# Weighting the one-hot rows of an expert router on ScalarE instead of VectorE, one block of eight tokens ahead

## The reference, cut to what matters

```python
q = (xt @ w_pq).reshape(T, PK_HEADS, 2, PK_DHALF)
s1, s2 = einsum('thd,hnd->thn', q[:, :, 0], k1), einsum('thd,hnd->thn', q[:, :, 1], k2)
t1, i1 = lax.top_k(s1, 16); t2, i2 = lax.top_k(s2, 16)
ts, ci = lax.top_k((t1[..., :, None] + t2[..., None, :]).reshape(T, 8, 256), 16)
e = take(i1, ci // 16) * 128 + take(i2, ci % 16)      # expert = (first key, second key)
g = softmax(ts)                                        # gate of each of the 128 choices
act = gelu(einsum('td,thkd->thk', xt, u_tab[e]))
out = einsum('thk,thkd->td', g * act, v_tab[e])
```

## Time and profile before

| what | us |
|---|---|
| runs of the kernel | 2574.62, 2577.2, 2577.13; median 2577.13 |
| the profiled execution: its own time | 2580.62 |
| the profiled execution: its span | 2578.8 |
| gate stage, from the first one-hot instruction of DVE to the last product of PE: from 1482 to 1864 | 382 |
| in it: busy time of DVE, PE, POOL, ACT | 377.6, 330.7, 215.5, 157.0 |
| down stage and end: from 1878 to 2579 | 701 |

### The profile page before, as it was taken

The page is one execution under the profiler, slowest core; times in us unless marked ns, Lnnn a source line. Parts: engine busy times, 40 slices in busy tenths (PEclk is TensorE's granted clock), DMA queues, the critical chain, the costliest instruction groups (busy, mean ns, idle before and its releaser), DMA issues.

```text
span 2578.8 us, 29605 instructions
## 1 busy us (share of the span) xinstructions
PE 2331.2 (90%) x11005; PEld 1786.0 (69%) x11005; DVE 1622.4 (63%) x2696; ACT 666.8 (26%) x1419; POOL 964.2 (37%) x552
## 2 busy tenths in 40 slices
PE   6699999899879999997897988888879999999996
PEld 6699977665457978997897888888834444444442
DVE  2376654444543222999889799999835555555555
ACT  2143520133322212242333344434300110001011
POOL 8455455400004424264656665555411111111110
PEclk9899999955689999998998999999989999999998
DMA  6323233300133213164666777777799999999994
GB/s 237 105 99 109 98 107 124 104 20 17 33 94 139 66 33 128 42 233 139 226 229 203 235 252 282 281 271 280 268 361 371 374 381 378 386 377 383 383 376 180
DMA packets 192546, 541.94 MB, mean 210 GB/s; under 512 B 17057, under 2 KB 116194, under 8 KB 158882
## 3 DMA queue, kind: packets, MB, share of 16 engines
q1 hardware_dynamic: 113024, 243.30, 27.5%
q0 software_dynamic: 27776, 201.40, 20.4%
q10 hardware_dynamic: 51618, 95.52, 10.3%
HBM read 472.18 MB, written 67.67 MB: 209 GB/s over the span
## 4 chain that ended last, share of the span: by engine, by line
PE 61%; DVE 27%; issue 5%; ACT 2%; DMA 2%; POOL 2%; SPq 1%; ACTq 0%; DVEq 0%; POOLq 0%
PE ps L949 24%; PE ps L579 17%; PE ps L904 6%; PE ps L696 5%; DVE yg L1887 3%; PE ps L729 3%; DVE hot L2030 3%; DVE ring L1879 2%; DVE hot L2032 2%; PE ps L558 2%; PE ps L779 2%; PE ps L733 1%; DMA ge<-ge_scratch 1%; SPq L446 1%; DVE xn L1529 1%
## 5 line engine op out<-in xcount | busy, mean ns | idle before, releaser
L949 PE MATMUL ps<-vraw,gf 128*128 128x512 f32 x1536 | 665.1, 596 | 19.0 <-DVE gf L2046 11.4
L949 PEld LDWEIGHTS ps<-vraw,gf 128*128 128x128 f32 x1536 | 293.0, 191 | 390.6 <-issue 372.6
L505 POOL DMA_INDIRECT ring<-uv,place_of x192 | 228.0, 1188 | 789.6 <-DVE yg L1887 783.1
L904 PE MATMUL ps<-actH,uH 128*128 128x384 f32 x1024 | 355.7, 347 | 57.9 <-POOL uL L497 45.5
L497 POOL TENSOR_TENSOR uL<-uraw,uH 128x1024 fp32r<-128x1024 f32 x128 | 332.6, 2616 | 100.6 <-ACT uH L1389 99.3
L487 POOL TENSOR_SCALAR wH<-raw 128x1024 fp32r<-128x1024 f32 x112 | 120.5, 1094 | 653.7 <-PE ps L579 500.7
L904 PE MATMUL ps<-actL,uH 128*128 128x384 f32 x1024 | 349.1, 341 | 0.0
L904 PE MATMUL ps<-actH,uL 128*128 128x384 f32 x1024 | 348.4, 340 | 0.0
L1887 DVE SCALAR_TENSOR_TENSOR yg<-ring,coef,yg 128x1024 f32<-128x1024 f32 x192 | 280.0, 1458 | 36.6 <-ACT coef L1442 36.5
L1879 DVE SCALAR_TENSOR_TENSOR ring<-ring,xn 128x1024 f32<-128x1024 f32 x192 | 267.5, 1394 | 43.4 <-DMA ring<-uv,place_of 42.7
L579 PE MATMUL ps<-actH,wH 128*128 128x288 f32 (+1 forms) x960 | 288.2, 300 | 6.8 <-DVE actL L1546 6.8
(11 more groups left out here) (286 smaller groups left out, 3298.2 us busy)
## 6 DMA issues: line engine op xcount, KB each, us to landing
uraw<-wu SPq DMA_DIRECT2D x128, 512.0 KB, 4.4
vraw<-wv SPq DMA_DIRECT2D x128, 512.0 KB, 7.9
raw<-wts SPq DMA_DIRECT2D x56, 1024.0 KB, 4.9
ge_scratch<-ge ACTq DMA_DIRECT2D x128, 192.0 KB, 4.2
c_scratch<-cst ACTq DMA_DIRECT2D x12, 2048.0 KB, 8.1
cg<-c_scratch SPq DMA_DIRECT2D x32, 768.0 KB, 13.5
ge<-ge_scratch SPq DMA_DIRECT2D x128, 192.0 KB, 8.7
xres<-x ACTq DMA_DIRECT2D x2, 2048.0 KB, 12.1
```

Source lines behind the costliest of these rows:

```text
L505: pool.indirect_dma_start(out=ring[:, s % RING, :], out_offset=None, in_=a["uv"], in_offset=bass.IndirectOffsetOnAxis(ap=place_of[:, s:s + ...
L904: mm = pe.matmul(bank(b, TD), lhs, rhs, start=k == 0 and w == 0, stop=k == KT - 1 and w == 2)
L949: mm = pe.matmul(bank(2 * i + half), gf[:, q % GF_RING, i * P:(i + 1) * P], vraw[:, q % V_RING, half * CHUNK:(half + 1) * CHUNK], start=q ...
```

## The change

The multiplication of `hot2` by the gates leaves DVE. ACT does it, one instruction per token, 128 x 128 elements with a scale per partition (`weigh_hot`). DVE signals the raw one-hot matrices of block g with a new semaphore, `place_ready`; `hot_ready`, on which PE waits, is now given by ACT. ACT does weigh_hot(g+1) at the place of block g, ahead of copy_gates(g) and of that block's coefficient(s). In all 48 DVE instructions go and 384 ACT instructions come. The wait of DVE for its own second comparison goes too.

```diff
+        def weigh_hot(g):
+
+            act.wait_ge(place_ready, g + 1)
+            for t in range(8):
+                row, tok = hot2[:, g % 2, t, :], 8 * g + t
+                ins = act.activation(row, row, ACT.Copy, scale=chosenT[:, 2, tok:tok + 1])
+            ins.then_inc(hot_ready, 1)
+
...
                     if hot_place(g) == h:
+                        if g == 0:
+                            weigh_hot(0)
+                        if g + 1 < HOTS:
+                            weigh_hot(g + 1)
                         copy_gates(g)
...
-            step.done(ve.tensor_tensor(hot2[:, g % 2], iota[:, :].unsqueeze(1).broadcast_to(shape),
-                                       chosenT[:, 1, now].unsqueeze(2).broadcast_to(shape), ALU.is_equal))
-            ve.tensor_tensor(hot2[:, g % 2], hot2[:, g % 2],
-                             chosenT[:, 2, now].unsqueeze(2).broadcast_to(shape), ALU.mult).then_inc(hot_ready, 1)
+            ve.tensor_tensor(hot2[:, g % 2], iota[:, :].unsqueeze(1).broadcast_to(shape),
+                             chosenT[:, 1, now].unsqueeze(2).broadcast_to(shape), ALU.is_equal).then_inc(place_ready, 1)
```

More of the change, by code:

```diff
@@ L388, in encoder_layer @@
         dot_ready acted_ready coef_ready acc_done gates_ready tile3_ready fold_ready folded
-        x2_in y_ready taken_up ss_in""".split()
+        x2_in y_ready taken_up ss_in place_ready""".split()
     (const_in, gain_in, gain_used, memx_in, x_in, ssq_clear, ssq_ready, var_ready, std_ready, xn_ready, acth_done,
@@ L397, in encoder_layer @@
      dot_ready, acted_ready, coef_ready, acc_done, gates_ready, tile3_ready, fold_ready, folded,
-     x2_in, y_ready, taken_up, ss_in) = [S(name) for name in names]
+     x2_in, y_ready, taken_up, ss_in, place_ready) = [S(name) for name in names]
     ck_in = [S(f"ck_in{j}") for j in range(2)]
```

## The result

| | median us | ratio to before, 95% interval |
|---|---|---|
| before | 2577.16 | |
| changed kernel | 2616.23 (2613.8 to 2622.66, 4 runs) | 1.0158 [1.0138, 1.0178] |
| the same again, on another occasion (the kernel before: 2576.40) | 2615.20 (2613.5 to 2616.64, 4 runs) | 1.0149 [1.0112, 1.0185] |

The change makes the kernel 39 us slower. The forecast was 2620, with a range of 2560 to 2645.

The account below looks back on a forecast made before the run. DVE was taken to bound the gate stage; the change makes a ring: 32 x 9.70 + 7 x 12.8 + 8 x 0.6 = 404.8 us, 43 us later, 2623.6 profiled, median 2620 us, range 2560 to 2645.

Parts of the forecast that it names:

- The bound before: Gate stage: DVE never waits; 5.48 us of own work plus 2.35 of POOL stalls make 7.83 us a block.
- The first rival: Gate stage: DVE stays full, ACT's chain hides, 6.58 us a block, -59 us, 2518; chance 0.07 together with the fourth rival.
- The scaling: ACT's eight gate multiplications a block: 0.30 us a token, 2.4 us a block; bounds 1.6 and 3.2.
- The ring: Gate stage: ACT's scaling waits for DVE's next comparisons, DVE's accumulate for ACT's coefficient behind it; 7.53 us without POOL stalls.
- Turn: One round of the ring, coefficient end to coefficient end: 7.53 plus one hit of 2.17, 9.70 us in short turns.
- The hits: POOL's `low` stretches a DVE comparison on the ring in every turn, 2.17 us each.
- two distances behind the coefficient: `low` starts 1.05 us (odd places) or 2.0 (even) after the coefficient's end, so a comparison is stretched.
- The second rival: Gate stage: the ring without hits, 330.5 us, -31 us, 2546; chance 0.18 for none to half hit.
- The sum: Gate stage: 32 short turns of 9.70, 7 long of 12.8 and eight DMA issues of 0.6 make 404.8 us.
- The 39 intervals: Gate stage: distances between the 40 steps' coefficients, 32 one block long and 7 two blocks, 404.8 us in all.
- The shift of the profiled execution: End of the gate stage: PE's last product starts 43 us later, and nothing behind gives this back or takes more.
- the slow start: PE in the gate stage: after waiting it starts slowly, some 2 us; stretches long turns by 1 to 2 us.

Follow-up runs that it names:

- experiment 5: Changed kernel with the multiplication by the gates left out on both engines, PE taking one-hot rows straight from DVE's comparisons: 2521.60 us, ratio 0.9779.
- experiment 1: Changed kernel with ACT's order at a block's place made copies, coefficient, then scaling of the next block; same work: 2529.18 us, ratio 0.9804.
- 6: Changed kernel with ACT's order at a block's place made coefficient, scaling of the next block, then copies: 2526.01 us, ratio 0.9805.
- experiment 2: Changed kernel with one added wait, so POOL's `low` starts only once DVE has compared the block after next: 2548.31 us, ratio 0.9882.
- 3: Changed kernel with every second token's scaling left out, so half the gates are not applied: 2569.86 us, ratio 0.9962.
- 7: Changed kernel with only the gate copies moved ahead of the scaling, the coefficient still last: 2588.74 us, ratio 1.0043.
- 4: Kernel before, DVE still multiplying, with ACT made to wait for DVE's next block ahead of its gate copies: 2599.91 us, ratio 1.0071.
- experiment 8: Changed kernel with ACT's order coefficient, scaling, copies, plus a wait holding `low` until DVE has compared the block after next: 2526.31 us, ratio 0.9809.

## Why the prediction was right

- **The bound before.** DVE full, 7.83 us a block by the sum, 7.84 measured. Taking the multiplication out gave 6.55 where the sum said 6.58 (experiment 5). The first rival, the naive gain, had the right price; what it lacked was the order on ACT. With the order of experiment 1 or 6 it nearly comes true, at 2526 to 2529 us.
- **The scaling.** 0.30 a token forecast, measured 0.387 long and eight in 2.44, with starts 0.29 apart. From the figures of the Trainium skill (ScalarE: Activation LUTs, What ACT_TABLE_LOAD costs) one is an estimated 186 + 0.833 x 128 + 93 = 386 ns; the trace's median of 387 agrees. The rule in the Trainium skill (ScalarE: Activation LUTs, Rules for kernel authors) to leave multiplications to VectorE named the right sign for the changed kernel, but the runs show that the cost on ScalarE is not what decides it: with all 384 scalings on ScalarE the kernel is 2% faster than before, if they stand behind the coefficient.
- **The ring.** Turn 9.65 against 9.70. Its sum without the hit was 7.53, and most short turns of experiment 2 take 7.45 to 7.47. Shown by cutting it (1, 6), by shortening it by known amounts (3: 1.17; 7: 0.97; 2: 2.2), and by making it in the kernel before (4).
- **The hits.** Their place on the ring was argued from two distances behind the coefficient. The trace shows `low` starting at 1607.42, 2.0 us behind a coefficient that ends at 1605.44, as worked out, at an odd place 1650.10, 1.03 behind one that ends at 1649.07 (forecast 1.05), and 40 of the 42 stretched instructions are comparisons. The prediction gave 2.17 for a hit without its source (its own row has 3.31 - 1.22 = 2.09); a turn of 9.65 less one of 7.46 makes it 2.19. Experiment 2 shows the price of them all: 68 us, where 32 x 2.17 is 69. The second rival is experiment 2 nearly to the microsecond, 2546 against 2548, and its stage, 330.5 us by the sum, took 330.5. The rival's own sign was misjudged a little: at -31 us without a hit the ring is slower from 31 / 2.17, about 14 hits on, not 11.
- **The sum.** The 39 intervals came to 400.0 us against 404.8. The shift of the profiled execution was 36.9 against 43: 3.4 of the difference lie in the stage, and 5.1 before it, as the first one-hot instruction started at 1476.9 instead of 1482.0, which the edit doesn't explain; the part behind the stage took 2.3 more. Over all eleven traces that first instruction starts anywhere from 1474.0 to 1482.0, so a few us of the whole are scatter from before the stage; the 400.0 against 404.8 is the better test of the account.
- **Where single forecasts were off.** I had DVE waiting 4 us a block on average and a busy share of 75%. The wait is 111.3 / 48 = 2.3 a block and 2.75 in the turn shown, since the dot fills 1.2 of the 3.97 from its own start to the accumulate's, a slip against my own ring; the share is 70%. PE's wait for the scaling was to be over 100 us and is 73.2: for the same work PE was busy for 349.6 us instead of 330.7, at a mean granted clock of 0.92 instead of 0.95. Part of that is the slow start: behind a wait of 3.41 us (1613.77) the product takes 2.51 to the next start, at a mean granted clock of 0.71, behind one of 1.73 (1604.12) it takes 1.80 at a granted clock of 1.00. How much of the 19 us this accounts for is open.

## What to carry to other kernels

Before moving work from a full engine to an idle one, write down what stands behind the new wait in the idle engine's queue, and ask whether the full engine waits for any of it. If it does, the two take turns instead of working side by side, however little either has to do; put what the other engine waits for ahead of the wait. Where two engines that are each far from full wait for each other by about the same amount, look for such a ring, and count what lies on it, stalls by a third engine too.

## What the runs showed of the hardware

A POOL `low` that starts while DVE is in an instruction with two inputs in SBUF lets that one end and stretches the next by about 2.2 us (3.42 against 1.22). `low` itself waits too: from the end of the DVE instruction in which it started to its own end it is 2.2 us both in the changed kernel (1607.90 to 1610.14) and in experiment 2 (1602.71 to 1604.91), though the whole takes 2.72 in one and 3.26 in the other.

What a hit costs depends on where it falls. Letting `low` run while DVE waits took the stretched instructions of the stage from 42 to 22 and the time down by 68 us (experiment 2). In a kernel in which DVE hardly waits the same edit moved the hits, 34 of 48 to the accumulate, and took nothing off (experiment 8). POOL's DMA_INDIRECT stretched neither of the two comparisons beside it.
